# Taps of a depthwise convolution in three places, an output chunk in parts, and scores moved into the middle of a half chunk

## The chip, the cores and the metric

One core of a Trainium2 chip runs the whole program. The metric is the device time of one execution in microseconds; the kernel is launched once and reads all weights from memory.

## The reference

Two models are run one after the other on a sequence of 256 tokens of width 1024, two layers each, in float32.

The first block (per layer) makes, from a normalised and modulated x (and, in layer 0, from a context of 256 more tokens), the projections `h @ w_in`; a convolution branch `silu(layer_norm(depthwise_conv(a * sigmoid(b), 31 taps))) * silu(gate) @ w_proj_a`; a neighbourhood attention and a window attention, both with context keys; and merges them: `y = sigmoid(g_a)*y_a + sigmoid(g_b)*y_b + sigmoid(g_c)*y_c`, `x = x + gate * (y @ w_o)`. Layer 0 carries 512 tokens (x and context), layer 1 carries 256.

The second block (per layer) is feed-forward, token mix, feed-forward, each with `x = layer_norm(DN_ALPHA * x + ...)`. The token mix has three attentions: one over compressed, selected and near keys (`_nsa`), one over a sliding window with sinks (`_swa_sink`), one with forget gates (`_fox`), and merges them with gates `sigmoid(h @ w_gate + b_gate)` and a last product `merged @ w_out`.

## The kernel before

**Weights.** All large weights come as a stream of chunks of 1 MB, 128 x 2048 in float32, in the order of their use. SyncE loads them into a ring of four. ScalarE (ACT) rounds each half of a chunk to `w_hi` (line 225), VectorE (DVE) makes the rest `w_lo` = ring - `w_hi` (line 239), each in two buffers. TensorE (PE) makes three products for each pair of operands, lines 281 to 283 (`w_hi`*`x_hi`, `w_hi`*`x_lo`, `w_lo`*`x_hi`). A chunk is 16 tiles of 128x128, so 48 matmuls; over 256 tokens they are 256 columns wide, over 512 tokens 512. `pe_half` makes PE wait until a half of the chunk is split. All matmuls of this program run on PE in the order of the code; the engines are ordered among each other by semaphores only, and each `nc.Block()` ends with all engines meeting.

**First block, per layer.** `glu_stage` (4 chunks) makes the convolution's padded input `cpad`; `qkv_stage` (9 chunks) makes queries, keys and values; `attend_both` runs 32 steps of attention in layer 0 and 16 in layer 1; `merge_stage` has 24 chunks of gates, merges and branch projections and 4 output chunks, and in layer 0 another 16 chunks of the modulation ("ada") woven in after main chunks 2 to 17. The convolution is done on DVE, one instruction for each tile of 128 channels and tap: 4 x 31 = 124 (`Conv.taps`, line 1424), in the order tap by tap over the four tiles. 92 of them stand in `qkv_stage`, shared out over its chunks behind the making of `w_lo`, and 32 in `attend_both`, shared out over its steps. `merge_stage` takes the mean over channels at main chunk 1 and the mean of squares at main chunk 4 (lines 990), and the normalisation follows.

At the output the first chunk needs y, whose parts (tiles 0-3, 4-5, 6-7) come late: `y_made` makes PE wait for each part while it goes through tile m=0 of the chunk. In front of k=4 PE runs padding matmuls that nobody reads, `keep_awake` (line 347; 10 in layer 0 of the first block, 6 elsewhere). The second block's last product does the same (`attend_and_merge`).

**Second block, attention.** Steps of attention are woven with half chunks by `woven(steps, halves)`. `attend_and_project` has 28 steps, 18 halves and 12 extra items of the forget gates (`Forget`); `attend_and_merge` has 20 steps over the first 26 halves. A step on PE is: the score of step t (`pe_score`, line 749), the turning of the probabilities of step t-2 (line 761) and the product with the values of step t-3 (line 774; both in `pe_rest`). `SplitSteps` issues the score at the step's own place and the rest in the middle of the half chunk that follows, after 12 of its 24 matmuls. The score of a step may start once DVE has read the one before it; there is one score buffer. On DVE a step (`a.dve`) waits for the score, adds the bias and takes the maximum (line 794), scales the probabilities of step t-1 (line 819), and may take an output. Each engine goes through the same list of items:

```python
for what, j, half in items:
    if what == "step":
        a.dve(dve, j)
        continue
    ...
    rest_behind(dve, j, half)
```

`rest_behind` in half q = 2j+half makes the `w_lo` of half q+1 (it counts `q = 2 * j + half - 1` from the chunk after). For the last projection chunk DVE makes, in this order: `w_lo` of the first half of output chunk 0, the lower part of y 0-3, the products and sums of that projection, the lower parts of y 4-5 and 6-7, and only then `w_lo` of the output chunk's second half. In `merge_stage` of the first block both halves come ahead of y's parts.

**Others that the change touches.** `pe_half_rows` (lines 1970 to 1972; chunks whose tokens are the rows of the result) waits for both halves of its chunk at the start. `project_and_compress` flattens keys and values for the compressed attention in 16 DVE instructions (line 2433) at chunk 3.

Of the kernel before, what the change touches and what calls it, by code (L numbers as in the profile page):

```python
# [26 lines left out]
P = 128  # L27
D = 1024
KT = D // P
# [86 lines left out]
def build(nc, wstream, xT, ctxT, cT, consts, vecs, rpb, rel, out):  # L116
    ctx = ExitStack()
    with ctx:
# [756 lines left out]
        def merge_stage(layer, branches, y, sg, prod, op_hi, op_lo, tok, take_out, halves):  # L875
# [47 lines left out]
            conv, squares = branches[2], y[:, 0:4, 0:tok]  # L923
# [47 lines left out]
            with nc.Block() as block:  # L971
# [13 lines left out]
                def _(pe):  # L985
# [7 lines left out]
                    for j, (kind, b, i) in enumerate(seq):  # L993
# [6 lines left out]
                        if k == 1:  # L1000
                            sum_tiles(0, lambda k: conv[:, k, 0:tok])
                        elif k == 4:
                            sum_tiles(3, lambda k: squares[:, k, :], lambda k: pe.wait_ge(squared.sem, q0 + k + 1))
                            pe.wait_ge(centred.sem, c0 + 4)
                        elif k == 7:
                            pe.wait_ge(rooted.sem, r0 + 1)
                        if later:
                            for turned_at, (_, which) in turns.items():
                                if k == turned_at + 2:
                                    pe.wait_ge(modulated.sem, o0 + 2 * which + 2)  # L1010
                        if k >= 2:
# [9 lines left out]
                        elif kind == "out":  # L1021
                            def y_made(k):
                                if k == 4:
                                    keep_awake(pe, 10 if later else 6, side(number[j]) + 1536)
                                if k in (0, 4, 6):
                                    pe.wait_ge(lower.sem, l0 + 3 * per_branch + (0, 4, 6).index(k) + 1)
                            pe_columns(pe, j // 2, j % 2, *model_operand(tok), tok, before=None if i else y_made, **place)
# [16 lines left out]
                def _(act):  # L1044
# [4 lines left out]
                    for j, (kind, b, i) in enumerate(seq):  # L1049
# [46 lines left out]
                        if k == 2:  # L1096
# [3 lines left out]
                        elif k == 4:  # L1100
                            act.wait_ge(step.sem, b0 + 2)
                            inverse_root(act, sums(3), rs[:, 0:tok], eps_col, r0)
                        elif k == 6:
# [13 lines left out]
                def _(dve):  # L1117
# [6 lines left out]
                    for j, (kind, b, i) in enumerate(seq):  # L1124
# [60 lines left out]
                        if k == 1:  # L1185
                            dve.wait_ge(step.sem, b0 + 1)
                            for k in range(4):
                                dve.tensor_tensor(conv[:, k, 0:tok], conv[:, k, 0:tok], sums(0), ALU.subtract
                                                  ).then_inc(centred.sem, 1)
                        elif k == 5:  # L1190
# [6 lines left out]
                        if kind == "out":  # L1197
                            take_out(dve, j, i, lambda m, w: out_of(j, S, m * tok + w * S))
# [38 lines left out]
        def block1(layer):  # L1237
            tok = 2 * S if layer == 0 else S
            sets = tok // S
            with ExitStack() as st:  # L1240
                conv_out = sb("conv_out", [P, 4, tok], stack=st)
                nq = sb("nq", [P, 4, tok], stack=st)
                wq = sb("wq", [P, 4, tok], stack=st)
                with ExitStack() as st5:
# [15 lines left out]
                    wv = rs[:].rearrange("p (a b) -> p a b", a=4)  # L1260
                    if layer == 0:
# [3 lines left out]
                    cpad = sb("cpad", [P, 4, 2, S + 2 * PAD], stack=st5, side="right")  # L1265
                    conv = Conv(layer, tok, cpad, conv_out)
                    with ExitStack() as st3:
                        glu_gate = sb("glu_gate", [P, 4, 2 * S], stack=st3)
                        glu_stage(layer, cpad, glu_gate, tok, model_norm(mods[layer], scales, scratch_of_x), na_bias)
                        qkv_stage(layer, tok, conv, nq, nk, nv, wq, wk, wv, glu_gate, st3)  # L1270
                    attend_both(layer, tok, conv, nq, nk, nv, na_bias, wq, wk, wv)
                with ExitStack() as st2:
                    y = sb("y", [P, KT, 2 * S], stack=st2)
                    sg = sb("sg", [P, 4, 2 * S], stack=st2)
                    prod = sb("prod", [P, 4, 2 * S], stack=st2)
                    sb("half_line", [P, HALF_LINE], stack=st2)
                    op_hi = sb("op_hi", [P, 4, 2 * S], F32R, stack=st2)
                    op_lo = sb("op_lo", [P, 4, 2 * S], F32R, stack=st2)
# [13 lines left out]
                    merge_stage(layer, (nq, wq, conv_out), y, sg, prod, op_hi, op_lo, tok, take_out,  # L1292
# [4 lines left out]
        def glu_stage(layer, cpad, glu_gate, tok, norm, na_bias):  # L1297
# [11 lines left out]
            with nc.Block() as block:  # L1309
# [33 lines left out]
                def _(act):  # L1343
                    norm.act(act)
                    for j in range(n):
# [4 lines left out]
                        if j < 2:  # L1350
                            wide = acc(j % 2, 1024 if j == 0 else 2 * tok).rearrange("p (m t) -> p m t", m=2)
                            for w in range(sets):
                                o = act.activation(cpad[:, 2 * j:2 * j + 2, w, PAD:PAD + S],
                                                   wide[:, :, w * S:w * S + S], ACT.Copy)
                                o.then_inc(acc_free.sem if w == sets - 1 else gpart.sem, 1)
# [6 lines left out]
                def _(pool):  # L1362
                    pool.memset(cpad[:, :, :, 0:PAD], 0.0)
                    pool.memset(cpad[:, :, :, PAD + S:], 0.0)
                    norm.pool(pool)

                @block.vector
                def _(dve):
                    norm.dve(dve)
                    for j in range(n):  # L1370
                        if j:
                            rest_next(dve, j // 2, j % 2)
                        if j >= 2:
                            m = slice(2 * j - 4, 2 * j - 2)
                            dve.wait_ge(acc_free.sem, g0[0] + j + 1)
                            for w in range(sets):
                                v = cpad[:, m, w, PAD:PAD + S]
                                dve.tensor_tensor(v, v, glu_gate[:, m, w * S:w * S + S], ALU.mult
                                                  ).then_inc(read.sem, 1)
# [14 lines left out]
            read.n += 2 * sets  # L1394
            if sets == 2:
                gpart.n += 2
            used(n)

        class Conv:
# [3 lines left out]
            LATER = 32  # L1403

            def __init__(self, layer, tok, cpad, out):
                self.tok, self.cpad, self.out = tok, cpad, out
                self.w, self.b = par(layer, "conv_w"), par(layer, "conv_b")
                self.order = [(ct, k) for k in range(CONV_K) for ct in range(4)]
# [3 lines left out]
            def taps(self, dve, first, end):  # L1412
                sets = self.tok // S
                for c in range(first, end):
                    ct, k = self.order[c]
                    src = self.cpad[:, ct, 0:sets, k:k + S]
# [5 lines left out]
                    else:  # L1422
                        dve.wait_ge(conv_step.sem, self.c0 + c - 3)
# [3 lines left out]
        def qkv_stage(layer, tok, conv, nq, nk, nv, wq, wk, wv, tmp, st):  # L1427
# [19 lines left out]
            here = CONV_K * 4 - Conv.LATER  # L1447
# [183 lines left out]
        def attend_both(layer, tok, conv, nq, nk, nv, na_bias, wq, wk, wv):  # L1631
# [3 lines left out]
            with ExitStack() as st:  # L1635
# [8 lines left out]
                with nc.Block() as block:  # L1644
# [6 lines left out]
                    def _(dve):  # L1651
                        cuts = [len(conv.order) - conv.LATER + round(conv.LATER * t / a.U) for t in range(a.U + 1)]
# [322 lines left out]
        class SplitSteps:  # L1975
# [50 lines left out]
        def attend_and_project(a, forget, plan):  # L2026
# [12 lines left out]
            with nc.Block() as block:  # L2039
# [85 lines left out]
        def attend_and_merge(a, branches, y, sg, prod, bias, moments):  # L2125
# [24 lines left out]
            with nc.Block() as block:  # L2150
# [5 lines left out]
                def _(pe):  # L2156
                    hi, lo = model_operand(S)
                    split = SplitSteps(pe, a)
                    for what, j, half in items:
# [12 lines left out]
                        elif kind == "out":  # L2172
                            def y_made(k):
                                if k == 4 and i == 0:
                                    keep_awake(pe, 6, 2048 * ((g0[0] + j) % 2) + 1536)
                                if k in (0, 4, 6) and i == 0:
                                    pe.wait_ge(lower.sem, l0 + (0, 4, 6).index(k) + 1)
                            apart = 512 if j == n - 1 else S
                            mm = pe_half_columns(pe, j, half, hi, lo, KT, lambda m: acc(j, S, apart * m), split.rest, y_made)
# [42 lines left out]
                def _(dve):  # L2222
# [6 lines left out]
                    def take(j):  # L2229
                        kind, b, i = seq[j]  # L2230
                        if kind == "out":
# [3 lines left out]
                                                     in1=acc(j, 2 * S).rearrange("p (m t) -> p m t", m=2),  # L2235
# [58 lines left out]
        def project_and_compress(layer, plan, norm, kkc, vc, v_b, gates, st):  # L2294
# [26 lines left out]
            with nc.Block() as block:  # L2321
# [100 lines left out]
                def _(dve):  # L2422
                    def flatten():
                        dve.wait_ge(doubled.sem, d0 + 32)
                        for w in range(4):
# [23 lines left out]
                    for j in range(n + m):  # L2449
# [13 lines left out]
                        if j == 3:  # L2463
# [385 lines left out]
```

## Time and profile before

| | us |
|---|---|
| median of 3 runs | 2486.89 (2480.13 to 2488.97) |
| the profiled execution | 2476.31 |
| its span, first to last instruction | 2473.3 |
| PE busy in the span | 2361.8 (95%) |
| DVE busy | 1485.9 (60%) |
| ScalarE busy | 1227.4 (50%) |
| GpSimd busy | 214.0 (9%) |
| mean granted clock of PE | 0.984 of full |
| read from memory | 346.15 MB, 140 GB/s over the span |

The profiled execution is one run; its own time stands 3.0 us above its span. A matmul's record is longer than the pace at which matmuls follow each other, so a busy PE can still lose time between starts.

### The profile page before, as it was taken

Reading aid. Unit: us, or ns where it says so; the run is one execution under the profiler, and the core shown is the slowest. Engines: PE = TensorE matmul, PEld = TensorE weight load, DVE = VectorE, ACT = ScalarE, POOL = GpSimd, SP = SyncE. Lnnn points to the kernel's source line nnn. Section 1 sums busy time; section 2 is a strip of 40 time slices with the busy share of each in tenths; the row PEclk is TensorE's granted clock in tenths of the full one; section 3 lists DMA queues with packets and bytes.
Section 4 is the critical chain, followed back from the end, with each engine's and each line's share of the span. In section 5 each row is a group of like instructions: output and inputs, shape, how many; then the busy total and the mean of one; then the engine's idle time right before and its main releaser. Section 6 shows DMA issues by size and latency. Waiting matters only on the chain. (4 is left out here: it accounts for less than half of the span.)

```text
span 2473.3 us, 45419 instructions
## 1 busy us (share of the span) xinstructions
PE 2361.8 (95%) x17496; PEld 2116.2 (86%) x17496; DVE 1485.9 (60%) x2687; ACT 1227.4 (50%) x1954; POOL 214.0 (9%) x228
## 2 busy tenths in 40 slices
PE   6998999999999899999989999999999989999998
PEld 4776577888788699999987889999999977899998
DVE  5379944443467955655466565664655666566554
ACT  6265745443347655434465454543544555555443
POOL 1022000000002000022000000221121000000220
PEclk9999999999999999999999999999999999999999
DMA  7321024343233045555452235455455542343552
GB/s 288 109 88 40 1 103 152 154 170 139 73 127 111 1 154 187 193 182 187 170 193 95 97 129 173 164 191 188 153 186 191 173 151 85 131 157 138 192 191 91
DMA packets 59444, 352.46 MB, mean 143 GB/s; under 512 B 6128, under 2 KB 17568, under 8 KB 18208
## 3 DMA queue, kind: packets, MB, share of 16 engines
q1 hardware_dynamic: 59152, 350.39, 39.9%
q8 instruction: 103, 1.69, 0.3%
q14 instruction: 45, 0.37, 0.0%
q10 hardware_dynamic: 144, 0.01, 0.0%
HBM read 346.15 MB, written 1.08 MB: 140 GB/s over the span
## 5 line engine op out<-in xcount | busy, mean ns | idle before, releaser
L239 DVE TENSOR_TENSOR w_lo<-ring,w_hi 128x1024 fp32r<-128x1024 f32 x638 | 807.8, 1299 | 486.9 <-ACT w_hi L225 486.7
L281 PE MATMUL psum<-x_hi,w_hi 128*128 128x256 f32 (+1 forms) x3376 | 1031.8, 306 | 17.4 <-PEq L1309 4.7
L283 PE MATMUL psum<-x_hi,w_lo 128*128 128x256 f32 (+1 forms) x3376 | 1011.6, 300 | 0.0
L282 PE MATMUL psum<-x_lo,w_hi 128*128 128x256 f32 (+1 forms) x3376 | 1010.4, 299 | 0.0
L225 ACT ACTIVATE w_hi<-ring 128x1024 fp32r<-128x1024 f32 (+1 forms) x638 | 643.7, 1049 | 308.7 <-PE psum L283 149.0
L281 PEld LDWEIGHTS psum<-x_hi,w_hi 128*128 128x128 f32 x3376 | 638.2, 189 | 61.5 <-issue 24.1
L282 PEld LDWEIGHTS psum<-x_lo,w_hi 128*128 128x128 f32 x3376 | 638.8, 189 | 26.6 <-issue 1.7
L283 PEld LDWEIGHTS psum<-x_hi,w_lo 128*128 128x128 f32 x3376 | 637.8, 189 | 23.2
L1796 PE MATMUL psum<-h_lo,w_hi 128*128 (+1 forms) x640 | 178.3, 279 | 0.0
L1797 PE MATMUL psum<-h_hi,w_lo 128*128 (+1 forms) x640 | 178.3, 279 | 0.0
L1794 PE MATMUL psum<-h_hi,w_hi 128*128 (+1 forms) x640 | 178.2, 279 | 0.0
L844 ACT ACTIVATE probT<-psum 128x512 f32<-128x512 f32 (+3 forms) x128 | 79.7, 623 | 179.0 <-PE psum L761 178.5
L1818 ACT ACTIVATE gate<-psum 128x256 f32<-128x256 f32 x88 | 33.8, 384 | 271.1 <-PE psum L283 271.1
L1869 POOL CAST h_hi<-hid 128x256 f32 (+1 forms) x88 | 35.0, 397 | 1296.9 <-DVE hid L1838 1296.9
L1424 DVE SCALAR_TENSOR_TENSOR conv_out<-cpad,vec,conv_out 128x512 f32<-128x512 f32 (+1 forms) x240 | 145.3, 662 | 0.0
L859 ACT ACTIVATE prob<-prob,neg 128x256 f32<-128x256 f32 (+6 forms) x256 | 127.9, 503 | 34.4 <-DVE neg L812 28.2
L1797 PEld LDWEIGHTS psum<-h_hi,w_lo 128*128 128x128 f32 x640 | 120.8, 189 | 0.0
L1794 PEld LDWEIGHTS psum<-h_hi,w_hi 128*128 128x128 f32 x640 | 120.8, 189 | 0.0
L1796 PEld LDWEIGHTS psum<-h_lo,w_hi 128*128 128x128 f32 x640 | 120.1, 188 | 0.0
L1838 DVE SCALAR_TENSOR_TENSOR hid<-psum,gate 128x256 f32<-128x256 f32 x88 | 37.3, 424 | 136.8 <-ACT gate L1818 136.6
L1871 POOL TENSOR_TENSOR h_lo<-hid,h_hi 128x256 f32 (+1 forms) x88 | 109.6, 1246 | 13.5 <-POOL h_hi L1869 12.7
L761 PEld LDWEIGHTS psum<-cst,prob 128*128 128x128 f32 (+1 forms) x544 | 61.5, 142 | 44.0 <-DVE prob L819 40.6
(307 smaller groups left out, 2862.1 us busy)
## 6 DMA issues: line engine op xcount, KB each, us to landing
ring<-wstream SPq DMA_DIRECT2D x320, 1024.0 KB, 4.8
x<-xT SPq DMA_DIRECT2D x2, 1024.0 KB, 7.5
x<-ctxT SPq DMA_DIRECT2D x2, 1024.0 KB, 9.8
rel_bias<-bias_by_distance SPq DMA_DIRECT2D x2, 1024.0 KB, 8.3
cst<-consts SPq DMA_DIRECT2D x1, 1534.0 KB, 12.1
wk<-wk_once SPq DMA_DIRECT2D x8, 128.0 KB, 4.2
kk_sw<-kk_sw SPq DMA_DIRECT2D x8, 128.0 KB, 5.9
out<-x SPq DMA_DIRECT2D x8, 128.0 KB, 2.0
```

What stands on the lines that cost most here:

```text
L225: act.activation(w_hi[:, c % 2, h], ring[:, (c + 2 * i) % RING, h], ACT.Copy).then_inc(hi_done.sem, 1)
L239: dve.tensor_tensor(w_lo[:, c % 2, h], ring[:, (c + 2 * i) % RING, h], w_hi[:, c % 2, h].bitcast(F32), ALU.subtract).then_inc(split_done.s ...
L281: pe.matmul(o, w_hi[:, c, w_cols], hi, start=first, stop=False)
L282: pe.matmul(o, w_hi[:, c, w_cols], lo, start=False, stop=False)
L283: return pe.matmul(o, w_lo[:, c, w_cols], hi, start=False, stop=last)
L844: act.activation(self.probT[0:w, v % self.TURNS, :, 0:n], psum[0:w, at:at + wide].rearrange("p (h k) -> p h k", h=2)[:, :, 0:n], ACT.Copy) ...
L859: o = act.activation(p, p, ACT.Exp, bias=self.neg[:, t % 3, half:half + 1], accum_out=self.den[:, t % 3, half:half + 1])
L1424: dve.scalar_tensor_tensor(out=o, in0=src, scalar=wc, in1=o, op0=ALU.mult, op1=ALU.add).then_inc(conv_step.sem, 1)
L1794: pe.matmul(o, w_hi[:, c, b:b + P], h_hi[:, kt, :], start=start and k == 0, stop=False)
L1796: pe.matmul(o, w_hi[:, c, b:b + P], h_lo[:, kt, :], start=False, stop=False)
L1797: mm = pe.matmul(o, w_lo[:, c, b:b + P], h_hi[:, kt, :], start=False, stop=False)
L1871: pool.tensor_tensor(h_lo[:, j, :], hid[:, s, :], h_hi[:, j, :].bitcast(F32), ALU.subtract).then_inc(lower.sem, 1)
```

## The change

- **Taps in three places.** `Conv` now goes tap by tap over tiles 0 to 2 (93 taps) and then through the 31 taps of tile 3. `qkv_stage` does 84 (layer 0) or 82 (layer 1), `attend_both` 9 or 26, `merge_stage` the last 31 or 16, in four portions behind main chunks 0 to 3. A tap waits for the one three before it, in tile 3 for the one just before it. The padded input of tile 3 has a place of its own that lives on into the merge. The mean over channels moves from main chunk 1 to 4, the mean of squares from 4 to 8, the wait for the inverse root from 7 to 12; the squares are kept in `prod`.
- **GLU.** Its copies and products go tile by tile; the memsets of the padding come after the casts on GpSimd.
- **First output chunk in parts.** `pe_in_parts` goes through k 0-3 for both m, then 4-5, then 6-7. The padding matmuls at k=4 are gone; two stand ahead of the chunk in the first block, none in the second.
- **Woven steps.** `SplitSteps` issues turns, values and then the score, all in the middle of the half chunk. Ahead of an extra item a pending step is flushed.
- **Row chunks.** `pe_half_rows` waits for its chunk's second half only at k=4.
- **Flatten** is done at chunks 2 and 3, eight instructions each.

```diff
+        def pe_in_parts(pe, j, hi, lo, before, out):
+            for part in (range(0, 4), range(4, 6), range(6, 8)):
+                for m in range(2):
+                    for k in part:
+                        if k == 0:
+                            pe_half(pe, j // 2, j % 2, m)
+                        if m == 0:
+                            before(k)
+                        mm = three(pe, out(m), slice((m * KT + k) * P, (m * KT + k + 1) * P), (g0[0] + j) % 2, hi(k),
+                                   lo(k), k == 0, k == KT - 1)
+            mm.then_inc(chunk_done.sem, 1)
...
@@ merge_stage, PE @@
-                        if k == 1:
-                            sum_tiles(0, lambda k: conv[:, k, 0:tok])
-                        elif k == 4:
-                            sum_tiles(3, lambda k: squares[:, k, :], lambda k: pe.wait_ge(squared.sem, q0 + k + 1))
-                            pe.wait_ge(centred.sem, c0 + 4)
-                        elif k == 7:
-                            pe.wait_ge(rooted.sem, r0 + 1)
+                        if k == 4:
+                            pe.wait_ge(conv_step.sem, taps_left.c0 + all_taps)
+                            sum_tiles(3, lambda k: conv[:, k, 0:tok])
+                        elif k == 7:
+                            pe.wait_ge(centred.sem, c0 + 4)
+                        elif k == 8:
+                            sum_tiles(8, lambda k: squares[:, k, :], lambda k: pe.wait_ge(squared.sem, q0 + k + 1))
+                        elif k == 12:
+                            pe.wait_ge(rooted.sem, r0 + 1)
...
-                                if k == 4:
-                                    keep_awake(pe, 10 if later else 6, side(number[j]) + 1536)
...
+                                keep_awake(pe, 2, side(k) + 1536)
+                                pe_in_parts(pe, j, *model_operand(tok), y_made, lambda m: out_of(j, tok, 512 * m))
...
@@ merge_stage, DVE, at the end of each main chunk @@
+                        if k < beside:
+                            taps_left.taps(dve, cuts[k], cuts[k + 1])
+                        elif k == beside:
                             dve.wait_ge(step.sem, b0 + 1)
...
-            LATER = 32
+            HERE = (84, 82)
+            LATER = (CONV_K, 16)
...
-                self.order = [(ct, k) for k in range(CONV_K) for ct in range(4)]
+                self.order = [(ct, k) for k in range(CONV_K) for ct in range(3)] + [(3, k) for k in range(CONV_K)]
...
-                        dve.wait_ge(conv_step.sem, self.c0 + c - 3)
+                        dve.wait_ge(conv_step.sem, self.c0 + c - (2 if ct < 3 else 0))
...
@@ pe_half_rows @@
             if t == 0:
                 pe_acc(pe, 0, j)
-                pe_half(pe, 0, j, 1)
...
             for k in range(KT):
+                if t == 0 and k % (KT // 2) == 0:
+                    pe_half(pe, 0, j, 2 * k // KT)
...
@@ SplitSteps @@
             def step(self, t):
                 self.rest()
-                self.a.pe_score(self.pe, t)
                 self.pending = t
 
             def rest(self):
                 if self.pending is not None:
                     self.a.pe_rest(self.pe, self.pending)
+                    self.a.pe_score(self.pe, self.pending)
                     self.pending = None
...
                         elif what == "extra":
+                            split.rest()
                             forget.pe(pe, j)
...
@@ attend_and_merge, PE @@
-                                if k == 4 and i == 0:
-                                    keep_awake(pe, 6, 2048 * ((g0[0] + j) % 2) + 1536)
...
+                            if i == 0:
+                                if half == 0:
+                                    pe_acc(pe, 0, j)
+                                    pe_in_parts(pe, j, hi, lo, y_made, lambda m: acc(j, S, 1024 * m))
+                                continue
...
@@ project_and_compress, DVE @@
-                        if j == 3:
-                            flatten()
+                        if j in (2, 3):
+                            flatten(range(2 * j - 4, 2 * j - 2))
```

## Rows read from the trace of the kernel before

**Rows 1.** The page: the span, and TensorE's busy time, share and instructions.

```profile
span 2473.3 us, 45419 instructions
...
PE 2361.8 (95%) x17496; PEld 2116.2 (86%) x17496; DVE 1485.9 (60%) x2687; ACT 1227.4 (50%) x1954; POOL 214.0 (9%) x228
```

**Rows 2.** Windows: layer 0's first attention; layer 0's second-block projections; its merges.

```profile
core 0: us, PE busy (x) PEld busy (x) DVE busy (x) ACT busy (x) POOL busy (x), PEclk, DMA share, GB/s
228.00:320.00 92.00, 82.81 (x704) 52.02 (x704) 85.92 (x312) 66.67 (x160) 0.00 (x0) 0.96 0.01 2
...
1295.00:1402.00 107.00, 98.04 (x782) 82.94 (x782) 62.71 (x253) 56.66 (x157) 0.00 (x0) 0.94 0.26 92
1402.00:1534.00 132.00, 131.56 (x1128) 122.37 (x1128) 78.96 (x201) 70.05 (x151) 0.00 (x0) 1.00 0.42 144
```

**Rows 3.** TensorE's waits: total us, times, the longest.

```profile
PE psum L761 <- DVE prob L819: 11.5, 13, 2.3
...
PE psum L749 <- PEq L1462: 8.3, 2, 6.0
PE psum L1970 <- DVE w_lo L239: 8.0, 4, 3.2
...
PE psum L326 <- DVE w_lo L239: 4.5, 2, 2.3
PE psum L749 <- DVE mx L794: 4.1, 13, 0.5
```

**Rows 4.** Timeline of a woven step, layer 0's merges: start us, length us.

```profile
1443.94 0.44 PE L749 MATMUL psum<-x_hi,qc 64*128 64x128 f32 x4
...
1444.42 0.39 PE L281 MATMUL psum<-qa,w_hi 128*128 128x256 f32 x1
1444.64 0.29 DVE L794 CUSTOM_DVE_ANT_0 prob<-psum,fox_bias 128x128 f32<-128x128 f32 x1 [1.72 <-PE psum L749]
...
1445.90 0.38 PE L761 MATMUL psum<-cst,prob 128*128 128x128 f32 x2
1446.12 1.22 DVE L239 TENSOR_TENSOR w_lo<-ring,w_hi 128x1024 fp32r<-128x1024 f32 x1
...
1446.80 0.39 PE L281 MATMUL psum<-qa,w_hi 128*128 128x256 f32 x1
...
1448.38 0.50 PE L749 MATMUL psum<-x_hi,qc 64*128 64x256 f32 x4
...
1448.93 0.38 PE L281 MATMUL psum<-x_hi,w_hi 128*128 128x256 f32 x1
```

**Rows 5.** Timeline: the start of the last row chunk, layer 0.

```profile
1389.42 1.22 DVE L239 TENSOR_TENSOR w_lo<-ring,w_hi 128x1024 fp32r<-128x1024 f32 x1
...
1390.79 0.36 PE L1970 MATMUL psum<-w_hi,x_hi 128*128 128x256 f32 x1 [3.17 <-DVE w_lo L239]
```

**Rows 6.** Timeline: first output chunk of the second block, layer 1.

```profile
2240.33 1.50 PE L347 MATMUL psum<-cst 128*128 128x128 f32 x12
...
2242.50 0.39 PE L281 MATMUL psum<-x_hi,w_hi 128*128 128x256 f32 x1 [0.67 <-DVE x_lo L2225]
...
2242.97 2.35 DVE L239 TENSOR_TENSOR w_lo<-ring,w_hi 128x1024 fp32r<-128x1024 f32 x2
...
2244.24 0.39 PE L281 MATMUL psum<-x_hi,w_hi 128*128 128x256 f32 x1
```

**Rows 7.** Timeline: first output chunk of the first block, layer 0.

```profile
624.24 0.39 PE L281 MATMUL psum<-x_hi,w_hi 128*128 128x512 f32 x1
...
625.61 2.39 PE L347 MATMUL psum<-cst 128*128 128x128 f32 x20
...
629.01 0.51 PE L281 MATMUL psum<-x_hi,w_hi 128*128 128x512 f32 x1 [1.01 <-DVE x_lo L1120]
```

**Rows 8.** Groups on DVE by form, around flatten, layer 0.

```profile
L2433 DVE TENSOR_TENSOR flat<-x,vec 64x120 f32<-64x120 f32 x16 | 5.0, 352 | 0.2
```

**Rows 9.** Taps of layer 0: the group in the attention; last run before it.

```profile
L1424 DVE SCALAR_TENSOR_TENSOR conv_out<-cpad,vec,conv_out 128x512 f32<-128x512 f32 x32 | 23.8, 744 | 0.0
...
218.75 8.84 DVE L1424 SCALAR_TENSOR_TENSOR conv_out<-cpad,vec,conv_out 128x512 f32<-128x512 f32 x10
```

**Rows 10.** Timeline of DVE: the operand's lower part, layer 0's first merge chunk.

```profile
354.01 2.35 DVE L1155 TENSOR_TENSOR op_lo<-nq,op_hi 128x1024 fp32r<-128x1024 f32 x2
```

More of the change, by code:

```diff
@@ L872, in attention_buffers, with merge_stage @@
                     *(sb(name, [P, 3, 2], stack=st, side=side) for name in ("mx", "den", "fac", "neg")))
-        def merge_stage(layer, branches, y, sg, prod, op_hi, op_lo, tok, take_out, halves):
+        def merge_stage(layer, branches, taps_left, y, sg, prod, op_hi, op_lo, tok, take_out, halves):
             main = []
@@ L921, in adds @@
                 return a0 + 4 * (b - 1) + 2 * h + piece + 1
-            conv, squares = branches[2], y[:, 0:4, 0:tok]
+            conv, squares = branches[2], prod[:, :, 0:tok]
+            beside = 4
+            all_taps = len(taps_left.order)
+            cuts = [taps_left.late + (all_taps - taps_left.late) * k // beside for k in range(beside + 1)]
             gains, biases = par(layer, "cln_g"), par(layer, "cln_b")
@@ L1260, in block1 @@
                     wv = rs[:].rearrange("p (a b) -> p a b", a=4)
+                    cpad = sb("cpad", [P, 3, 2, S + 2 * PAD], stack=st5, side="right")
                     if layer == 0:
@@ L1264, in block1 @@
                         na_bias = sb("na_bias", [P, NA_COLS + 256], stack=st5, side="right")[:]
-                    cpad = sb("cpad", [P, 4, 2, S + 2 * PAD], stack=st5, side="right")
-                    conv = Conv(layer, tok, cpad, conv_out)
+                    pads = [*(cpad[:, ct] for ct in range(3)), last_pad]
+                    conv = Conv(layer, tok, pads, conv_out)
                     with ExitStack() as st3:
                         glu_gate = sb("glu_gate", [P, 4, 2 * S], stack=st3)
-                        glu_stage(layer, cpad, glu_gate, tok, model_norm(mods[layer], scales, scratch_of_x), na_bias)
+                        glu_stage(layer, pads, glu_gate, tok, model_norm(mods[layer], scales, scratch_of_x), na_bias)
                         qkv_stage(layer, tok, conv, nq, nk, nv, wq, wk, wv, glu_gate, st3)
@@ L1351, in _ @@
                             wide = acc(j % 2, 1024 if j == 0 else 2 * tok).rearrange("p (m t) -> p m t", m=2)
[L1352 to L1355, printed above, removed]
+                            for m in range(2):
+                                o = act.activation(pads[2 * j + m][:, 0:sets, PAD:PAD + S],
+                                                   wide[:, m, 0:tok].rearrange("p (w t) -> p w t", w=sets), ACT.Copy)
+                                o.then_inc((gpart, acc_free)[m].sem, 1)
                         else:
@@ L1373, in _ @@
                         if j >= 2:
-                            m = slice(2 * j - 4, 2 * j - 2)
                             dve.wait_ge(acc_free.sem, g0[0] + j + 1)
[L1376 to L1379, printed above, removed]
+                            for m in (2 * j - 4, 2 * j - 3):
+                                v = pads[m][:, 0:sets, PAD:PAD + S]
+                                dve.tensor_tensor(v, v, glu_gate[:, m, 0:tok].rearrange("p (w t) -> p w t", w=sets),
+                                                  ALU.mult).then_inc(read.sem, 1)
                         if j in (1, 2):
@@ L1651, in _ @@
                     def _(dve):
-                        cuts = [len(conv.order) - conv.LATER + round(conv.LATER * t / a.U) for t in range(a.U + 1)]
+                        cuts = [conv.here + (conv.late - conv.here) * t // a.U for t in range(a.U + 1)]
                         for t in range(a.length):
@@ L2422, in _, with flatten @@
                 def _(dve):
-                    def flatten():
+                    def flatten(which):
                         dve.wait_ge(doubled.sem, d0 + 32)
-                        for w in range(4):
+                        for w in which:
                             pe_ = par(layer, "pe_k" if w < 2 else "pe_v")
```

65 lines of the change are left out of this document (37 added, 28 removed).

## The prediction

> **What bounds the kernel now.** The page comes first: TensorE (PE) is busy 2361.8 of 2473.3 us [rows 1], so a gain must shorten PE's own work or its waits, and anything that makes PE wait is paid in full. Second, the windows by stage: PE is full (131.6 of 132 us) where the layer's last three branches are merged, and has holes in the first block's attention (82.8 of 92) and in the projections beside the first attention steps (98.0 of 107); VectorE (DVE) is nearly full (85.9) only in the first block's attention [rows 2]. Third, the list of waits shows what the holes wait for: scaled probabilities from DVE 11.5 us, the start of the attention after the last taps 8.3, row chunks on their rounded-off weights `w_lo` 8.0 and, in another stage, 4.5, and a score on its buffer 4.1 [rows 3]. All that the change can win is in these and in the padding matmuls of keep_awake. Last, the timeline of one woven step, to see how much room the moved score has [rows 4].
>
> **The woven step, by which the sum is decided.** On DVE the order of items is not edited: `a.dve(t)` blocks on the score of step t, and the `w_lo` half that PE needs for its *next* half chunk is queued behind it (rest_behind at half q makes half q+1). The trace shows that pairing: a row chunk that needs its second half at once stands still 3.17 us until the `w_lo` made in the same item ends [rows 5].
> Before: the score starts at 1443.94, PE's matmuls resume at 1444.42, DVE starts on the score at 1444.64 and its `w_lo` ends at 1446.12+1.22=1447.34, 2.92 us after PE resumed. PE needs it at 1448.93 [rows 4]. Slack 1.59 us, and no wait; the step takes 1448.93-1444.42=4.51 us.
> After: PE runs 12 matmuls (1445.90-1444.42=1.48), turns and values (1446.80-1445.90=0.90), the score (0.48), 12 matmuls (1448.38-1446.80=1.58), and wants the next half. The score ends 1.48+0.90=2.38 us later in the step than before, more than the slack. DVE's 2.92 us now stand against 1.58 us of PE. The step becomes the loop 1.48+0.90+0.48+2.92=5.78 us, 1.27 longer. The one change of array form that is saved is already in this (matmuls to score cost PE about 0.2 us start to start where 0.12 is the pace; the loop does not need it).
> The list woven(20, 26) has 16 scoring steps, each directly ahead of a half; the first has its next half made already. 15 x 1.27 x 2 layers = **+38 us**. Bounds: 0 (less 16 x 2 x 0.18 of form changes = -6) if DVE's lower half were ahead, and 1.6 x 30 = +48 if each also carried the 0.4 us of a taken pair. I take the measured step.
>
> **The projections beside the first steps** (28 steps, 18 halves, 12 extras). An extra now first flushes the pending step, so its half has nothing in its middle and `w_lo` is not late. But in four places two steps stand together ahead of an extra (3, 9, 17, 23): turns of step t want probabilities that DVE scales after score t-1, and that score was issued just before; DVE needs 1446.12-1444.42=1.7 us for it [rows 4]: 4 x 1.6=6.4. In some seven more only 12 matmuls (1.48) and the like cover it: 7 x 0.4=2.8. Less: the waits for the score's buffer, 4.1 over both layers, mostly go (-1.9 a layer), and 24 x 0.18=4.3 of form changes. +3 a layer, **+6** (bounds -10 and +20).
>
> **Row chunks by halves.** Chunks 7 and 8 of that stage wait 4.0 us a layer for the second `w_lo` half [rows 3, 5]; it is now wanted after 12 matmuls (1.48). Of the four waits (8.0) two are the 3.17 kind, so the other two are (8.0-6.3)/2=0.8 and go whole; of the long ones about 0.7 stays won after the later steps: **-3** (bounds -5, 0).
>
> **First output chunk in parts.** In block 1 PE runs 20 padding records from 625.61 and resumes at 629.01: 3.4 us lost [rows 7]. Six matmuls take 625.61-624.24=1.37, so one 0.23; the first four k of both m are 24 of them, 5.5 us, instead of 2.75, so y's second part is there; two padding matmuls (0.5) are added: -2.9. Layer 1 has the padding of rows 6, whose loss is 2242.50-2240.33=2.2, and gets the same 0.5: -1.7. Together **-4.6**; if a second part of y were late by what is late now (1.0 and 0.7), -2.9; if nothing is added by the two matmuls, -5.6.
> In the second block the same edit meets DVE's order: `w_lo` of the chunk's second half comes after the last products, sums and lower parts of y. PE reaches that point at 2240.33 and the second half is there at 2244.24, which in the trace is where its 24 remaining matmuls begin (0.33 late) [rows 6]. In parts, m=1 is asked for at 2240.33: nothing runs until 2244.24, and 36 matmuls remain instead of 24: 12 x 0.12=1.4, x 2 = **+2.8**.
>
> **Flatten in two places.** 16 operations of 0.352 us [rows 8] stand ahead of the `w_lo` for which PE waits 2.25 us in each layer [rows 3]. Half of them, 2.8 us, move one chunk ahead; the `w_lo` of either chunk is then late by nothing or by 0.5 at most, since PE is at a chunk of 48 matmuls (5.8 us) against two halves (2.4), a lower part and 2.8 of flatten on DVE: **-4.6**, bounds 0 and -4.6. Should the doubling transfer that flatten waits for land late, DVE would block there a chunk sooner: that is the 0.
>
> **Taps.** A 512-wide tap is 744 ns [rows 9]. Layer 0: 8 fewer in the nine projection chunks is one fewer in the last run of ten (8.84 us), which alone sets the start of the attention: -1.3. In the attention 9 instead of 32: every four steps DVE sheds 4 x 23/32 x 0.744=2.1 us and PE becomes the bound there; it idles 92.0-82.8=9.2 us in that stage, mostly in the waits for probabilities [rows 2, 3], and these go: -9. In the merge 7 or 8 taps stand behind the op_lo pieces and ahead of the `w_lo` of the next chunk's second half: per pair of main and modulation chunk DVE has five halves (6.1), op_lo (2.35) and 8 taps (5.9)=14.4 us, PE 48 x 0.23 + 16 x 0.12=12.9 [rows 4, 7, 9, 10]. That gives one wait in a chunk and one for the last tap ahead of the mean: +5 (bounds 0, +10). Layer 1 (82, 26, 16): -0.6-1.5+1.7. Together **-6**. The squares and the inverse root move past a few chunks and keep their length, and what wants them (k 8 and 12) moves with them, so nothing. The depthwise copies and memsets by tile (GLU stage) lie under PE's chunks; 0 to +0.3.
>
> **Clock.** Stages with holes have a mean granted clock of 0.94 and 0.96, full ones 1.00 [rows 2]; 0.94 of 107 us is 12.8 us at the lower of the two levels. The two new stalls of 3.9 us should bring about one such spell each: **+2**.
>
> Sum: 38+6-3-4.6+2.8-4.6-6+2 = **+31**. On the profiled execution (2476.31, span 2473.3) that is 2507; the median of the three runs is 10.6 above it, so 2486.89+31=2518, of which I give 2517.
>
> **Rivals.**
> *Clock falls in the merges too* (0.18). For: 30 new stalls of 1.3 us put these 132 us where the projections are now (PE 92% busy, clock 0.94); against: the first attention, 90% busy, keeps 0.96. Price: 132 x 0.06=8 us a layer lost, +16, 2533. [...]
> *The stall is half as large* (0.12). If DVE's stretch shrinks to 2.25 us (no scaling wait, short blocks), the loop adds 0.6: 18 instead of 38, 2498, within 0.5%.
> *DVE is not late* (0.17), the other side. If the weight half were finished within the 1.58 us after the score, through an order of DVE's work that I misread, 38 becomes -6 and the sum -13: 2473. It decides where the added step time is under 0.25 us. Against it: the 3.17 us wait [rows 5].
> *The forecast* (0.53), own range 2503 to 2531.
> What a measurement can tell from no change is about 0.5%. Slower 0.71, same 0.12, faster 0.17. The range 2472 to 2544 leaves out about half of the faster case and the worst clock.
>
> **What the profile after would show.** In the waits a new leader, matmuls of block 2's merges waiting for `w_lo` some 30 times by 1.2 us or more; the windows of those stages about 150 instead of 132 us; DVE's idle before the score longer; L326's wait gone; the attention of layer 0 near 83 us; a 3.9 us hole at the first output chunk of the second block, none in the first. I am wrong if PE's next half starts without a wait after a score, or if the first merge loses more than 10 us to taps.

## The result and the profile after

| | before | after |
|---|---|---|
| median | 2483.51 us (2479.89 to 2488.97, 4 runs) | 2544.12 us (2542.89 to 2549.98, 4 runs) |
| ratio | | 1.0248, 95% interval 1.0231 to 1.0264 |
| profiled execution, span | 2476.31, 2473.3 us | 2542.89, 2541.1 us |
| mean granted clock | 0.984 | 0.979 |

The change makes the kernel some 61 us slower; 31 was forecast. The head of the page after:

```profile
span 2541.1 us, 45344 instructions
...
PE 2377.2 (94%) x17448; PEld 2127.0 (84%) x17448; DVE 1490.7 (59%) x2689; ACT 1234.9 (49%) x1960; POOL 212.8 (8%) x240
```

TensorE's (PE's) busy time rose by 15 us [rows 1] with 48 matmuls fewer, and its idle time by 52. Where this happened is seen in windows of whole stages, each from the stage's first matmul to the first of the next. Kernel before: projections and merges of layer 0, the same of layer 1, and last the first block's attention of layer 0.

```profile
core 0: us, PE busy (x) PEld busy (x) DVE busy (x) ACT busy (x) POOL busy (x), PEclk, DMA share, GB/s
1295.50:1402.10 106.60, 97.99 (x782) 82.89 (x783) 62.57 (x252) 56.64 (x157) 0.00 (x0) 0.95 0.26 92
1402.10:1556.00 153.90, 153.16 (x1309) 143.75 (x1310) 93.88 (x220) 79.43 (x160) 0.00 (x0) 1.00 0.43 151
2004.90:2110.20 105.30, 96.67 (x784) 81.95 (x784) 62.51 (x253) 56.66 (x157) 0.00 (x0) 0.96 0.27 94
2110.20:2264.10 153.90, 153.17 (x1308) 143.72 (x1309) 93.82 (x220) 79.43 (x160) 0.00 (x0) 1.00 0.42 151
227.90:320.30 92.40, 82.90 (x704) 52.14 (x705) 85.92 (x312) 66.67 (x160) 0.00 (x0) 0.96 0.01 2
```

Kernel after, the same stages, with the attention first:

```profile
227.40:316.90 89.50, 81.05 (x705) 50.98 (x705) 72.63 (x289) 65.83 (x160) 0.00 (x0) 0.98 0.01 2
1293.10:1403.80 110.70, 98.35 (x783) 83.77 (x783) 62.47 (x253) 57.44 (x158) 0.00 (x0) 0.92 0.26 89
1403.80:1585.10 181.30, 156.36 (x1297) 145.74 (x1298) 93.41 (x220) 80.46 (x160) 0.00 (x0) 0.98 0.35 128
2033.20:2147.30 114.10, 101.70 (x783) 86.49 (x783) 62.47 (x253) 57.44 (x158) 0.00 (x0) 0.90 0.25 86
2147.30:2329.60 182.30, 157.54 (x1296) 146.84 (x1297) 93.53 (x219) 80.47 (x160) 0.00 (x0) 0.97 0.36 128
```

The merges of the second block lost 27.4 and 28.4 us, the projections ahead of them 4.1 and 8.8: together 68.7, where the span grew by 67.8. In all other stages gains and losses cancel. The list of PE's waits over the whole program names what is waited for (total us, times, longest):

```profile
PE psum L281 <- DVE w_lo L239: 39.3, 29, 3.7
PE psum L776 <- DVE prob L834: 23.9, 24, 1.8
PE psum L353 <- DVE c_both L408: 10.5, 1, 10.5
...
PE psum L281 <- DVE y L2290: 9.5, 4, 2.5
...
PE psum L764 <- PEq L1497: 6.5, 2, 4.6
```

The first line stood at 2.3 us in 2 waits before; of its 29 waits 24 are in the two merges (16.3 us in each, 3.7 of them the hole at the output chunk). L776 and L764 are L761 and L749 of before [rows 3]; of the second line 15.0 us are in the two projections, which had none before. One woven step of the merges after, PE and DVE (line 764 is the score, 809 its reading, 842 the taking of an output):

```profile
1460.61 0.36 PE L281 MATMUL psum<-x_hi,w_hi 128*128 128x256 f32 x1 [1.10 <-DVE w_lo L239]
...
1462.10 0.60 PE L776 MATMUL psum<-cst,prob 128*128 128x128 f32 x4
1462.63 0.44 PE L789 MATMUL psum<-probT,v_b 128*64 128x128 f32 x4
1463.00 0.50 PE L764 MATMUL psum<-x_hi,qc 64*128 64x256 f32 x4
...
1463.77 0.42 DVE L809 CUSTOM_DVE_ANT_0 prob<-psum,fox_bias 128x256 f32<-128x256 f32 x1 [3.30 <-PE psum L764]
...
1465.06 0.42 DVE L842 TENSOR_TENSOR x_lo<-psum,x_hi 128x256 fp32r<-128x256 f32 x1
1465.39 1.22 DVE L239 TENSOR_TENSOR w_lo<-ring,w_hi 128x1024 fp32r<-128x1024 f32 x1
1466.66 0.39 PE L281 MATMUL psum<-x_hi,w_hi 128*128 128x256 f32 x1 [1.43 <-DVE w_lo L239]
```

The loop is there as forecast: a half starts at 1460.61, its score is issued 2.39 us later, DVE stands idle 3.30 us for it, and only behind it makes the `w_lo` that PE has needed since 1465.2. The step takes 1466.66-1460.61=6.05 us: the 5.78 on record and 0.27 more, in a step in which DVE also takes an output (0.42 us). Where DVE also makes the products of a projection chunk (line 2290), it is worse:

```profile
1469.09 0.44 PE L764 MATMUL psum<-x_hi,qc 64*128 64x128 f32 x4
...
1470.95 1.22 DVE L239 TENSOR_TENSOR w_lo<-ring,w_hi 128x1024 fp32r<-128x1024 f32 x1
1472.08 1.28 DVE L2290 SCALAR_TENSOR_TENSOR y<-sg,psum 128x512 f32<-128x512 f32 x2
1473.28 1.22 DVE L239 TENSOR_TENSOR w_lo<-ring,w_hi 128x1024 fp32r<-128x1024 f32 x1
...
1473.42 0.39 PE L281 MATMUL psum<-x_hi,w_hi 128*128 128x256 f32 x1 [2.17 <-DVE y L2290]
```

Here the next chunk also needs the products that free its accumulator, and they stand behind the late `w_lo`: 2.17 us.

### The profile page after: what moved, and what is told of

Its sections match the earlier page's. It is cut to its first block and busy times, and to the rows that moved or that the text cites. A ratio compares the mean times of both kernels' runs of the same rounds, so it can differ in the third digit from the quotient of the medians.

```text
span 2541.1 us, 45344 instructions
## 1 busy us (share of the span) xinstructions
PE 2377.2 (94%) x17448; PEld 2127.0 (84%) x17448; DVE 1490.7 (59%) x2689; ACT 1234.9 (49%) x1960; POOL 212.8 (8%) x240
## 5 line engine op out<-in xcount | busy, mean ns | idle before, releaser
L776 PE MATMUL psum<-cst,prob 128*128 128x128 f32 (+1 forms) x544 | 85.5, 283 | 25.9 <-DVE prob L834 23.9
L776 PEld LDWEIGHTS psum<-cst,prob 128*128 128x128 f32 (+1 forms) x544 | 59.3, 140 | 58.8 <-DVE prob L834 49.6
```

The lines of the kernel that those rows point to most:

```text
L776: mm = pe.transpose(self.turn(v, half, a)[0:w], self.prob[:, v % self.PROBS, half, a:a + w], const("ident"))
```

## Experiments

Each is the kernel before with the parts named, or the kernel after where that is said. Stage times are read from one trace of each kernel; in a second trace of the kernel before (`before_again`) the projections take 106.4 and 106.6 us and the merges 153.9 and 153.3, so differences of a microsecond say nothing.

**The woven step alone** (`woven_only`): only `SplitSteps` and the flush (a pending step is finished first) ahead of an extra item.

> The kernel before with the woven part alone (turns, values and score in the middle, flush ahead of an extra). If the late weight half is the cause, this run has nearly all of the loss: the two merge stages 181 instead of 154 us each, less the 1.4 us of the output chunk in parts, and the projections 4 to 9 longer each: ratio 1.022 to 1.026, and some 29 waits of matmuls for w_lo. If instead a good part of the loss is in the first block's taps or in the pace of other stages, the ratio is 1.015 or less.

2561.25 us, ratio 1.0307 (1.0285 to 1.0329): +76. That is more than the whole change costs, and above the range given. Merges 179.2 and 178.7 us (before 153.9 in both layers), projections 117.9 and 119.9 (before 106.6 and 105.3): these four stages alone account for +76.0. The projections, layers 0 and 1:

```profile
1299.20:1417.10 117.90, 102.19 (x782) 86.80 (x783) 62.51 (x253) 57.47 (x158) 0.00 (x0) 0.90 0.24 83
2050.50:2170.40 119.90, 103.71 (x782) 87.57 (x782) 62.58 (x253) 57.66 (x158) 0.00 (x0) 0.88 0.24 82
```

**All but the woven step** (`all_but_woven`).

> The changed kernel with the score back at the step's own place. Late weight half as the cause: the merges return to 154+1.4 us and the projections to 105 us, ratio 0.995 to 1.001 (the rest is -6.7 in the compressed attention's stages, -5 in the attentions, +8 in the first block's merges, +3 in the second block's output chunks, and 0 or +5 for the pace of the down projections). If the rest of the change costs in its own right: above 1.005.

2473.55 us, ratio 0.9956 (0.9945 to 0.9967): -11, within the range given. Merges 156.7 and 158.3 us, projections 102.3 and 102.1. With the run above -11+76=+65, where the whole shows +61 (57 to 66): the two halves of the change nearly add.

**The lower half made first** (`dve_ahead`): the kernel after, PE's order untouched, but on DVE the `w_lo` of the next half goes ahead of the step that blocks on the score:

```diff
-                    for what, j, half in items:
+                    for what, j, half in weights_first(items):
                         if what == "step":
                             a.dve(dve, j)
...
+                        elif what == "rest":
+                            rest_behind(dve, j, half)
```

> The changed kernel, but VectorE makes the weight half that the next half chunk needs ahead of the step that it would block on, in both woven stages; TensorE's order is as in the changed kernel. If the wait is VectorE's order and nothing else, the waits for w_lo in the merges go and the loss with them: merges at 150 to 156 us, ratio 0.99 to 1.00. If the later score itself makes the chain of a step too long, or the form changes and the clock are the cause, merges stay above 165 us and the ratio above 1.01.

2497.01 us, ratio 1.0053 (1.0035 to 1.0071): 47 of the 61 us are gone, somewhat fewer than expected. Merges 158.7 and 158.9 us, 3 above the range given and far below the 165 of the other reading. What waits are left in those of layer 1:

```profile
PE psum L281 <- DVE w_lo L239: 3.7, 1, 3.7
PE psum L281 <- DVE y L2305: 2.7, 2, 1.4
PE psum L281 <- DVE x L2305: 1.0, 1, 1.0
```

So in the merges the score's place costs little by itself, 2.0 and 0.6 us against `all_but_woven`; that the `w_lo` stands behind it cost 22.6 and 23.4. The one wait of 3.7 is the output chunk in parts. In the projections it is otherwise: they take 109.4 and 112.2 us here, 7.1 and 10.1 more than in `all_but_woven`, and PE waits 8.9 and 8.8 us there for scaled probabilities (11 times a layer), which `all_but_woven` never does. DVE's order doesn't cure this part. It is 17.2 of the some 24 us by which this kernel is slower than that one.

**Score first in the middle** (`score_before_turns`): as `woven_only`, but score, turns, values.

```diff
                 if self.pending is not None:
+                    self.a.pe_score(self.pe, self.pending)
                     self.a.pe_rest(self.pe, self.pending)
-                    self.a.pe_score(self.pe, self.pending)
```

> The kernel before, with the score, then turns, then values, all in the middle of the half chunk (an extra still flushes). The score is now issued 1.48 us later in its step than in the kernel before, where in the change it is 2.38 us later (behind turns and values too). Theory (the loop score, VectorE, w_lo, next half closes in a length that grows with what PE runs ahead of the score): the loop is 1.48 + 0.48 + 2.92 = 4.9 us where the step of the kernel before takes about 4.5 to 4.9, so the last three branches take 154 to 162 us a layer, near the 154 of the kernel before and far from the 181 of the change. Rival (what costs is that the score stands in the middle at all, or the flush ahead of the extras, or the clock): they stay at 175 us or more. Total, with the projections as slow as in the change or a little better: 2490 to 2512 us by the theory, 2540 or more by the rival.

2505.01 us, ratio 1.0088 (1.0063 to 1.0112), the total as expected. Merges 165.3 and 165.4 us, 3 above the range given, far from the rival's 175. With the score later by 0, 1.48 and 2.38 us in its step the merges take 153.9, 165.3 and 179.2 us in layer 0. The loop of 4.88 us gives 15 x 0.37=5.6 of the 11.4 us at 1.48; PE's waits for `w_lo` and for the products are 7.8 there, and the rest wasn't traced. DVE's idle time ahead of the score's reading (two groups, here of the 1.48) grows with the delay:

```profile
L794 DVE CUSTOM_DVE_ANT_0 prob<-psum,fox_bias 128x128 f32<-128x128 f32 (+1 forms) x16 | 5.2, 356 | 21.4 <-PE psum L749 21.3
...
L794 DVE CUSTOM_DVE_ANT_0 prob<-psum,rel_bias 128x128 f32<-128x128 f32 (+1 forms) x16 | 5.1, 356 | 22.3 <-PE psum L749 22.3
```

It is 27.6 us before, 43.7 here and 58.0 in `woven_only`.

**The second block's output chunk alone** (`parts2_only`), and the same **with padding** (`parts2_padded`):

```diff
+                        if k == 0 and m == 1:
+                            keep_awake(pe, 14, 2048 * ((g0[0] + j) % 2) + 1536)
                         if k == 0:
                             pe_half(pe, j // 2, j % 2, m)
```

> The kernel before, with the first output chunk of the second block alone in parts. Theory of record: PE stands still 3.9 us ahead of tile m=1, where it had padding matmuls and a small hole, and has 36 matmuls behind it instead of 24: +1.4 us a layer, +2.8 us in all, ratio 1.001. Rival: the hole also lowers the clock of what follows in both layers, +5 to +8 us, ratio 1.002 to 1.003.

> The kernel with the second block's first output chunk alone in parts, and in it 14 calls of padding matmuls ahead of tile m=1, in the 3.9 us for which TensorE stood still there (6 calls took 1.50 us in the kernel before, so 14 take 3.5 us). The order of the real matmuls is that of the run without the padding. That run cost 3.5 us a layer where the order alone accounts for 1.4. Theory (the hole itself is paid a second time, by the clock, which was 0.87 and 0.93 over the 26 us around it): with the padding the granted clock there is 1.00 and the last three branches take 155 to 156 us a layer, where that run has 158.0 and 156.7 and the kernel before 153.9; total ratio 1.000 to 1.002. Rival (something else in the order in parts costs the rest): they stay at 157 us or more, ratio 1.003 to 1.005.

Without padding 2492.88 us, ratio 1.0039 (1.0023 to 1.0054), above both ranges given; with it 2485.16, ratio 1.0016 (0.9998 to 1.0034), as expected. The intervals of the ratios overlap; the stage decides. Merges 158.0 and 156.7 us without, 155.3 and 155.5 with padding, 153.9 before: the order costs 1.5 a layer, as forecast (1.4), and PE's silence in the hole another 2.7 and 1.2. Layer 0 without padding, ahead of the hole, in it, and behind it:

```profile
1520.00:1530.60 10.60, 10.60 (x92) 10.60 (x91) 5.87 (x6) 4.54 (x6) 0.00 (x0) 1.00 0.47 186
1530.60:1534.60 4.00, 0.25 (x3) 0.05 (x2) 3.90 (x7) 3.12 (x4) 0.00 (x0) 0.90 0.00 0
1534.60:1541.60 7.00, 7.00 (x36) 7.00 (x37) 2.17 (x2) 0.00 (x0) 0.00 (x0) 0.57 0.78 301
1541.60:1551.60 10.00, 10.00 (x87) 10.00 (x86) 6.30 (x9) 4.02 (x4) 0.00 (x0) 1.00 0.30 106
```

Behind one stall of 3.9 us PE stands mostly at 1.2 GHz and gets 36 matmuls done in 7 us; at the 87 in 10 of the last line it would be 61, so 2.9 us are lost. In layer 1 it is 48 matmuls in 7 us at a granted clock of 0.79. With padding the whole stage shows a granted clock of 1.00. The Trainium skill (TensorE: Matmul & The Clock Gate, Part 1: The HAM clock gate) has TensorE fall to half rate after an idle spell and come back after sustained work; this hole and its padding agree.

**Three parts** (`three_parts`): output chunk of the first block, row chunks, flatten; nothing else.

> The kernel before, with the first output chunk of the first block in parts, the row chunks by halves and flatten in two places; taps, woven steps and the second block's output chunk as before. On record -4.6 - 3 - 4.6 = -12 us. What the stages of the run with all but the woven step showed: -2.7 or more (output chunk, layer 0), -3.4 and -2.4 (flatten), -2 to -3 (row chunks). So 2472 to 2476 us where the kernel before has 2485, ratio 0.995 to 0.9965; if the taps that are left out here had won something by themselves, it would be slower than the run with all but the woven step (0.9956), else as fast or faster.

2462.67 us, ratio 0.992 (0.9899 to 0.9941): -20, more than the 12 expected, and the fastest kernel of the study, ahead of before and after. Stages: first block's merge -2.7 (layer 0) and -0.6 (layer 1), compression with flatten -3.7 and -2.7, projections -4.0 and -3.4, together -17.1; stages that it does not touch were some 3 us shorter in this trace, of which the last section speaks. It is also some 10 us ahead of `all_but_woven`, whose further parts cost 6.9 (second block's output chunk) and 2 (taps) by the runs here. The page's head:

```profile
span 2453.4 us, 45371 instructions
```

Layer 1's -0.6 hides a gain, for the pace of matmuls in that stage differs by 0.8 us between two traces of the same kernel (167.2 and 168.0). At the output chunk itself PE went from 2.2 us of padding and wait in the kernel before

```profile
1013.59 1.50 PE L347 MATMUL psum<-cst 128*128 128x128 f32 x12
...
1015.76 0.38 PE L281 MATMUL psum<-x_hi,w_hi 128*128 128x256 f32 x1 [0.68 <-DVE x_lo L1120]
```

to two short pieces in `three_parts`:

```profile
1010.59 0.60 PE L362 MATMUL psum<-cst 128*128 128x128 f32 x4
...
1014.18 0.38 PE L281 MATMUL psum<-x_hi,w_hi 128*128 128x256 f32 x1 [0.16 <-DVE x_lo L1137]
```

From the last matmul ahead of the chunk to the chunk's last it takes 6.5 us instead of 7.9 (`before_again`, at the same pace; 7.8 in the first trace of the kernel before).

**Taps** (`taps_only`), and **no tap beside the attention** (`no_taps_in_attention`):

```diff
-            HERE = (84, 82)
-            LATER = (CONV_K, 16)
+            HERE = (93, 93)
+            LATER = (CONV_K, CONV_K)
```

> The kernel before with the taps in three places alone (with the tiles' places and the GLU stage that belong to it). From the trace after: attention -2.9 and -2.4, ends of the projections -1.3 and -0.7, first block's merges +6.6 and +5.6 (before the gain of the output chunk in parts): together +5, ratio 1.002, anywhere from 1.000 to 1.004. My forecast had -6, that is 0.9975.

> The change's taps alone, but with all 93 taps of tiles 0 to 2 beside the projections and none beside the attention (HERE 93 and 93, LATER 31 and 31). It tells what the waits of layer 0's attention are. My forecast on record: VectorE's load sets that stage's time, so with fewer taps the stage falls by 9 us, to 83 us. Rival: the waits are the latency of one step's chain (score, maximum, exponent, scaling, turn), which no tap lengthens; then the stage stays at 88 to 91 us with no tap in it at all, VectorE far from full.

Taps alone: 2486.76 us, ratio 1.0008 (0.9997 to 1.002), as expected and no gain. Layer 0's attention takes 91.2 instead of 92.4 us, its merge up to the output 6.9 us more, with these waits at its start:

```profile
PE psum L281 <- DVE w_lo L239: 3.5, 2, 3.2
```

Layer 1: attention -3.0, merge +3.2. With no tap in the attention at all (one run, 2498.37 us, in which layer 1's merge, now with 31 taps, is 12.9 us longer than before) layer 0's attention still takes 90.7 us:

```profile
228.60:319.30 90.70, 82.59 (x704) 52.00 (x704) 67.40 (x280) 65.82 (x160) 0.00 (x0) 0.96 0.01 2
...
PE psum L761 <- DVE prob L819: 6.7, 8, 2.1
```

DVE is idle for 23 of 91 us and PE waits eight times for scaled probabilities all the same (9 times, 7.8 us, in the kernel before). The waits are not DVE's load.

**The kernel before once more** (`before_again`).

> The kernel before once more, for a second trace of it. In its trace the 256-column matmuls of some stretches of 25 to 75 us follow each other at 113 ns and those of all others at 118 ns (31% of them at 113 ns, worth some 17 us), and every other kernel of this study had its own such stretches. If code placement decides, the same stretches are fast again; if it is chance of the execution, others are. The span is within 0.4% of 2473.3 us either way.

2479.42 us, span 2476.9, within the 0.4% expected. What it says of the pace is in the last section.

## Why the prediction was right and wrong

The sign and the main mechanism were right; the size was half. The steps that failed are the price of the clock, put at +2, and the term of the projections, +6 where they show +26. By the prediction's own terms, in us (measured: stages of the runs with that part alone, or without the others, layers 0 and 1 together):

| term | forecast | measured |
|---|---|---|
| woven step, merges | +38 | +50.1 |
| woven step, projections | +6 | +25.9 |
| row chunks | -3 | -7.4 |
| output chunk, first block | -4.6 | -4.1 |
| output chunk, second block | +2.8 | +6.9 |
| flatten | -4.6 | -6.4 |
| taps | -6 | +2 (-1 to +5), by the whole time |
| clock | +2 | inside the terms above |
| sum | +31 | +67 (the whole change: +61) |

- **The woven step in the merges.** The chain score, maximum, scaling, `w_lo`, next half was read rightly from [rows 4, 5], and `dve_ahead` shows it by taking its last link out. From one score to the next it is 5.27 us before and 6.84 after (mean of all fifteen intervals of layer 0; 6.92 in layer 1): +1.57 and +1.65 where 1.27 was on record. Over the first seven intervals of layer 0 it is +1.26, which is the forecast's step met where little else happens. What was missing are the six places where the next chunk also waits for products (y 9.5 and x 4.3 us after, 2.3 each where 1.2 is usual: 6.6 in all), and the clock.
- **The clock's price is the term that failed: +2.** (1 - granted clock) x length is 5.3 and 4.2 us for the projections before, nothing for the merges; after it is 8.9, 11.4, 3.6 and 5.5. That is 20 us more. Some of it falls into holes and costs nothing: where one sums, from start to start, how much longer than at full clock the matmuls in the half-rate spells took, these four stages lost 8.7 us before and 23.2 after, 14.5 more. The same sum in `parts2_only` puts 4.2 of them behind the two holes at the output chunk, so 10.3 are left for the short stalls. The forecast had priced only the two stalls of 3.9 us and taken the 30 short ones as free. The rival of the falling clock put 16 into the merges alone; by the product they show 9, the projections 11. What one short stall costs in clock was not measured by itself.
- **The projections.** In `woven_only` PE's idle time there rose by 14.7 us (8.6 a layer before, 15.7 and 16.2 then), as forecast: 2 x (6.4+2.8-1.9)=14.6. Its busy time rose by 11.2 us, and there the forecast had taken 8.6 off for changes of array form that are saved. No row of the prediction shows that saving's 0.18 us a change, and no run shows the saving. The two differences, 11.2 and 8.6, are the 20 us by which the term was missed. Summed from start to start, 13.9 us are matmuls at the lower clock.
- **The second block's output chunk:** the order's 1.4 us a layer was right (1.5); the padding that it takes away was counted as waste, and it had kept the clock up.
- **The first block's:** layer 0 -2.7 of -2.9, layer 1 -1.4 of -1.7 at the chunk itself: right.
- **Row chunks and flatten** won 13.8 where 7.6 was on record. The waits for the second `w_lo` half (4.0 us a layer) are gone, and what is left in their place are waits of 1.1 (for `x_lo`) and 0.3 us a layer, where 2.5 was forecast. Flatten removes its 2.25 us wait and gets back some clock (the stage's 0.95 became 0.98 in layer 0).
- **Taps.** -9 for layer 0's attention was wrong at its root: [rows 2] showed DVE full and PE waiting for DVE's probabilities, and that was taken for cause. A fifth of DVE's work can go (85.9 to 67.4 us) and 1.7 us are won. What bounds the stage instead, most likely the latency of a step's chain from score to turned probabilities, was not tested. The merge's +5 for layer 0 was 7.
- **The other side** (DVE not late) is excluded by the 24 waits in the merges, and the stall half as large by the step's length.

## What to carry to other kernels

Before an instruction that another engine waits for is moved later on its own engine, look at what that waiting engine has queued behind the wait: here 2.38 us later in a step with 1.59 us of slack cost 50 us over 30 steps in the merges, and putting one `w_lo` ahead of the wait gave 46 back. What the other engine must deliver to the moved work itself, as the probabilities in the projections, no such order gives back. A stall on TensorE has two prices, its length and the slow matmuls behind it; padding that looks like waste can be the cheaper of the two. Many short stalls pay the second price too, here some 10 us. A full engine that another waits for isn't yet the bound: take work off it in a run of its own before counting on the gain.

## What the runs showed of the hardware

**Matmuls at full clock have two paces.** With a granted clock of 1.00 and PE busy throughout, 50 us hold 443 or 427 matmuls of 256 columns (113 and 118 ns from start to start). Kernel before, three of the four loops of the feed-forward's second product, which share their code (the third, the fourth and the second in time):

```profile
1885.00:1935.00 50.00, 50.00 (x444) 50.00 (x443) 23.06 (x20) 18.73 (x19) 0.52 (x1) 1.00 0.57 203
2402.00:2452.00 50.00, 50.00 (x443) 50.00 (x442) 22.45 (x20) 19.38 (x19) 0.00 (x0) 1.00 0.35 127
1690.00:1740.00 50.00, 50.00 (x427) 50.00 (x426) 21.16 (x19) 18.09 (x18) 0.00 (x0) 1.00 0.53 189
```

The same program in a second execution (`before_again`):

```profile
1885.00:1935.00 50.00, 50.00 (x444) 50.00 (x443) 22.79 (x19) 19.09 (x20) 0.74 (x1) 1.00 0.56 204
2404.00:2454.00 50.00, 50.00 (x427) 50.00 (x426) 21.17 (x19) 19.12 (x19) 0.00 (x0) 1.00 0.35 127
```

The third loop is fast in both executions, the fourth in one of two. So the code alone doesn't decide; whether chance alone does, two executions can't tell, and the cause stays open. It is worth some us: the change's trace has none of its four down-projection loops at the fast pace, before has two, 2.1 us each (480 matmuls in 54.3 instead of 56.4 us). The Trainium skill (TensorE: Matmul & The Clock Gate, Back-to-back issue gap) gives an isolated matmul at full clock its columns over 2.4 GHz and about 2.5 ns, which by estimate is 109 ns here, and says that in a stream of weight loads and matmuls both set the spacing. Both paces of these loops lie above the 109.
